# Three of the seven score tiles counted by signs on ScalarE in the search for the top-256 threshold

## The reference, cut to what matters

```python
score = jnp.where(admissible[None], score, NEG)
_, sel = lax.top_k(score, top_k)          # top_k = min(256, L // 4) = 256
k_sel, v_sel = _gather_rows(keys, sel), _gather_rows(vals, sel)
...
p = jax.nn.softmax(logits, axis=-1)
```

## Time and profile before

| what | value |
|---|---|
| median of three runs | 1867.98 us |
| the profiled execution's own time | 1866.54 us |
| its span, first to last instruction | 1864.7 us |
| busy: PE, DVE, ACT, POOL | 1761.9, 1216.4, 774.3, 372.8 us |
| mean granted TensorE clock | 0.984 |
| column tiles on TensorE | 164.9 to 469.5 us |
| the search | 165 to 346.6 us |
| q, k and v | 470 to 641 us |

### The profile page before, as it was taken

How to read it: one execution, slowest core, us unless ns; L and a number is a source line. 1 busy time by engine, 2 the same in 40 slices (tenths; PEclk the granted TensorE clock), 3 DMA queues, 4 the chain that set the end, 5 groups by cost and what they waited for, 6 DMA issues and landing times.

```text
span 1864.7 us, 30284 instructions
## 1 busy us (share of the span) xinstructions
PE 1761.9 (94%) x11736; PEld 1586.3 (85%) x11736; DVE 1216.4 (65%) x2156; ACT 774.3 (42%) x1664; POOL 372.8 (20%) x451
## 2 busy tenths in 40 slices
PE   6977999999999987998999999999999999999999
PEld 6935999999889854667988789999999999887877
DVE  4279898999999666765453577555565554444443
ACT  5377566412566267664122443322222222333332
POOL 2104322331784122330000001111111112000000
PEclk9999999999999998998999999999999999999999
DMA  6411112321212423784332213222222222657574
GB/s 199 72 54 35 46 40 82 108 94 62 81 52 69 148 63 132 256 282 189 134 119 79 79 52 93 73 72 72 71 77 72 77 72 94 214 173 237 174 239 154
DMA packets 92881, 209.23 MB, mean 112 GB/s; under 512 B 13333, under 2 KB 32693, under 8 KB 92483
## 3 DMA queue, kind: packets, MB, share of 16 engines
q1 hardware_dynamic: 86555, 193.26, 32.4%
q10 hardware_dynamic: 6192, 14.16, 1.9%
HBM read 167.77 MB, written 39.58 MB: 111 GB/s over the span
## 4 chain that ended last, share of the span: by engine, by line
PE 40%; issue 14%; DVE 3%; ACT 2%; DMA 1%; POOL 1%; SPq 1%; POOLq 0%; DVEq 0%; ACTq 0%
PE ps L823 12%; PE ps L825 12%; PE ps L824 12%; DVE buf L1678 1%; DMA buf<-f_scr 1%; PE ps L1071 1%; PE ps L1048 1%; ACT buf L1484 1%; DVE buf L2243 1%; DVE buf L1877 0%; PE ps L1061 0%; PE ps L1105 0%; PE ps L1090 0%; SPq L791 0%; ACT buf L1474 0%
## 5 line engine op out<-in xcount | busy, mean ns | idle before, releaser
L825 PE MATMUL ps<-buf,buf 128*128 128x288 f32 (+3 forms) x2660 | 877.1, 330 | 0.0
L824 PE MATMUL ps<-buf,buf 128*128 128x288 f32 (+3 forms) x2660 | 877.1, 330 | 0.0
L823 PE MATMUL ps<-buf,buf 128*128 128x288 f32 (+3 forms) x2484 | 828.5, 334 | 24.9 <-DVE buf L1678 17.5
L825 PEld LDWEIGHTS ps<-buf,buf 128*128 128x128 f32 (+1 forms) x2660 | 500.9, 188 | 24.5
L824 PEld LDWEIGHTS ps<-buf,buf 128*128 128x128 f32 (+1 forms) x2660 | 501.5, 189 | 23.6
L823 PEld LDWEIGHTS ps<-buf,buf 128*128 128x128 f32 (+1 forms) x2484 | 467.9, 188 | 53.1 <-DVE buf L1678 15.3
L1678 DVE TENSOR_TENSOR buf<-buf,buf 128x512 fp32r<-128x512 f32 (+5 forms) x363 | 322.4, 913 | 196.8 <-ACT buf L1669 123.9
L1825 DVE SCALAR_TENSOR_TENSOR buf<-buf,buf,buf 128x1024 f32<-128x1024 f32 x240 | 197.9, 866 | 4.0
L2390 POOL TENSOR_TENSOR buf<-buf,buf 128x288 f32<-128x288 f32 x88 | 78.9, 900 | 416.8 <-DVE buf L2113 375.2
L1764 DVE TENSOR_SCALAR_CACHE_REDUCE buf<-buf,buf 128x384 uint8<-128x384 f32 (+6 forms) x169 | 139.8, 888 | 1.2
L1005 PE MATMUL ps<-buf,buf 128*128 128x256 f32 x432 | 124.5, 288 | 0.6 <-ACT buf L1366 0.6
(11 more groups left out here) (202 smaller groups left out, 1949.4 us busy)
## 6 DMA issues: line engine op xcount, KB each, us to landing
buf<-in_w_ffn SPq DMA_DIRECT2D x66, 512.0 KB, 3.6
buf<-in_w_ffn SPq DMA_DIRECT2D x88, 256.0 KB, 2.7
buf<-in_cache_k SPq DMA_DIRECT2D x16, 1024.0 KB, 7.4
buf<-in_cache_v SPq DMA_DIRECT2D x16, 1024.0 KB, 10.5
f_scr<-buf SPq DMA_DIRECT2D x22, 576.0 KB, 4.2
buf<-f_scr SPq DMA_DIRECT2D x66, 192.0 KB, 3.9
buf<-in_w_cols SPq DMA_DIRECT2D x24, 512.0 KB, 3.9
buf<-in_x SPq DMA_DIRECT2D x18, 512.0 KB, 4.3
```

The source lines that it names most:

```text
L823: mm(dst, whi, xhi, start=start, stop=False)
L824: mm(dst, whi, xlo, start=False, stop=False)
L825: return mm(dst, wlo, xhi, start=False, stop=stop)
```

## The change

`NSIGN` becomes 3 and is defined earlier; three small vectors get three columns in place of two. So the tile of 896 keys (block 6) goes from VectorE's list to ScalarE's. ScalarE sums signs over 896, 1024 and 1152 keys in each of the 32 steps, VectorE counts over 384, 512, 640 and 768. After the last bit VectorE handles three tiles in lines 1791 to 1800, not two.

```diff
+        NSIGN = 3
...
-        kvec = take(2, o + 32)
-        diff = take(2, o + 40)
-        least = take(2, o + 48)
-        assert NSEL <= 8 and o + 50 <= o_gmix + D
+        kvec = take(NSIGN, o + 32)
+        diff = take(NSIGN, o + 40)
+        least = take(NSIGN, o + 48)
+        assert NSEL <= 8 and o + 48 + NSIGN <= o_gmix + D
...
-        NSIGN = 2
         signed = list(enumerate(select))[NSEL - NSIGN:]
```

## The result

The changed kernel takes 1870.04 us against 1867.51 (medians of 20 runs each): ratio 1.0014, 95% interval 1.0008 to 1.002, so 1.5 to 3.7 us slower. Forecast were 1871.1 us and a loss of 3.1. The profiled execution took 1870.4 us with a span of 1868.6, against 1866.54 and 1864.7.

What follows compares the result with a forecast made beforehand. TensorE was taken to bound the column stage, with ScalarE's lag using up the PSUM banks. Its 3.1 us loss, everything else costed at nothing, added to the 1867.98 median gives 1871.1 us; own range 1869.5 to 1873, wider range 1865.5 to 1877.

Steps and rivals of the forecast that it cites:

- What bounds the stage: Column stage: TensorE sets it, 25.2 us a GLU pair; ScalarE's lag just uses up six PSUM banks near 335 us.
- The cost of a sum: ScalarE, each search step: third sum over 896 keys adds 1.04 us plus a 0.12 gap, 1.16 us.
- Steps a, b, d and e: GLU pair's steps: a 3.26 to 4.42, b 4.80 to 4.42, d 4.74 to 4.42, e 10.06 to 11.22 us.
- the collision of c: GLU pair's third step: threshold update no longer falls beside GpSimd's low part, so 6.26 becomes 5.11 us.
- The loss of 3.1 us: Column tiles: TensorE loses 3.1 us once, in two or three small waits for ScalarE's late evacuations; bounds 0 and +8.
- step a of tile 8, at 281.84, stays where it is: Tile 8's first step: starts unmoved after four GLU pairs and takes 5.2 us beside GpSimd's product, as before.
- the first pair: First pair of GLU tiles: changes by -0.5 us, an estimate with bounds -1 and +1.2.
- rival 2: GLU pairs: update still meets GpSimd, c costs 7.4 us, a pair 2.8 more; 1876 to 1878 us, chance 0.2.
- The tail: VectorE after the last bit: some 2.9 us more work, masks and taps about 5.8 us later, covered, costing nothing.
- Rival 1: Column tiles: the lag is absorbed, evacuation at 335.18 late by less than 1; 1868.0 to 1868.9 us, chance 0.15.
- rivals 3 and 4: 3: later VectorE meets GpSimd less, 1864 to 1868, chance 0.1; 4: by occupancy, search 12 us shorter, 1867.5, chance 0.08.
- The signs: Expected: c at 5.1, VectorE waiting every step, copies ending about 307.6; wrong if a later stage changes over 1 us.

Runs made afterwards that it cites:

- kernels 3 and 8: Against the kernel before: 3, two tiles by signs in the search, three after the last bit, 1866.22 us; 8, that with its final count done twice, 1867.36 us.

## Why the prediction was right, step by step

- **What bounds the stage.** That TensorE sets it, with a reserve of six banks that is used up near 335 us, held: every kernel that eased ScalarE went to 304.4 to 305.4 us and has no wait for an evacuation left, and the one that burdened it further grew by 33.
- **The cost of a sum**, 1.04 us plus 0.12, held (1039 ns; sums start 1.17 apart). Steps a, b, d and e were right within 0.02 us, c within 0.09; the collision of c is gone, as worked out from the order.
- **The loss of 3.1 us** stands against 4.17 in the profiled stage, of which 0.8 is TensorE's clock at the start, so some 3.4 for the change (an estimate, by the first evacuations), and against 1.5 to 3.7 for the whole. The term that was wrong is "step a of tile 8, at 281.84, stays where it is", with its a step "5.2, as before". Tile 8 began 0.46 late: the first pair gained nothing (34.46 us from the first sum, against 34.16), where I had put -0.5. The missing 0.8 is the clock: the evacuation of 193.22 shown above waited 0.96 us for TensorE, and all that followed in the pair came after it. With the clock of the kernel before the pair would have gained some 0.5, as forecast (an estimate). What the forecast had wrong is the first step of tile 8, which took 6.05 us. With three sums the update came at 286.83, in the middle of GpSimd's product (285.98 for 2.40), and the first of its three instructions took 1.56 us:

```profile
286.83 1.56 DVE L1780 TENSOR_TENSOR buf<-buf,buf 128x3 f32<-128x3 f32 x1 [1.48 <-ACT buf L1350]
288.43 0.39 DVE L1781 TENSOR_SCALAR buf<-buf 128x3 int32<-128x3 f32 x1
288.85 0.17 DVE L1783 SCALAR_TENSOR_TENSOR buf<-buf,buf 128x7 int32<-128x7 int32 x1
```

  So rival 2 was right in kind at one place of one tile: 0.8 us. With the 0.5 by which tile 8 began late it makes the 1.3 us that the copies after tile 9 were later than forecast (2.44, not 1.16), and weight tile 12 took 0.2 longer to come; the gate steps gave 0.3 back. That the sum came so near is in part luck: the 0.8 of this meeting was not foreseen, and small gains in the second to fourth pair and in the gate steps (some 0.7 together) make up for most of it.
- **The tail** was sized at 2.9 us and took 5.3 more (19.89 us from the last update to the masks, against 14.62): four tiny operations stood beside GpSimd for 0.58 to 0.67 each, the first raise took 1.12. VectorE's first weight piece was 9.7 us late and not 5.8. It cost nothing, for the cover was large: the second piece started at 495.83, and by the last copy of the convolution (636.69 against 631.26) VectorE was 5.43 us late, as late as TensorE at its next stage (647.71 against 642.29). That kernels 3 and 8 lose nothing shows it.
- **Rival 1** fell with the stage, rivals 3 and 4 too: TensorE's waits for GpSimd in q, k and v went from 7.1 to 6.9 us, and the search ends at 350.67, 4.1 later, where the rule of occupancy gave 12 earlier. (In the earlier trace rows TensorE has the highest occupancy of all, 29.12 of 29.12 us, and it did bound the stage; the rule misled only in the choice between the two engines that hand the steps to each other.) The busy times of the pair, in the columns of the earlier trace rows, look like balance, with VectorE at 18.94 us and ScalarE at 22.68; but by the timeline ScalarE hardly waits for the update, and VectorE waits in every step.

```profile
200.35:229.85 29.50, 29.50 (x171) 29.50 (x171) 18.94 (x60) 22.68 (x39) 8.44 (x10) 1.00 0.13 36
```

- **The signs.** Most came: c took 5.02 us, VectorE waited in all 32 steps, and the copies after tile 9 ended at 309.53 (forecast 307.6, with 0.71 of it from the later start). One sign of being wrong came as well, a later stage that gives more than 1 us. After a pause of 2.08 us at the end of the product with the output weights, TensorE's clock falls in some executions and not in others. The stretch in the kernel before, in the changed one, and in the changed one again:

```profile
1065.40:1070.40 5.00, 4.96 (x19) 4.27 (x20) 5.00 (x5) 3.14 (x6) 0.00 (x0) 0.66 0.38 105
1072.10:1077.10 5.00, 4.95 (x26) 4.20 (x27) 5.00 (x5) 3.16 (x6) 0.00 (x0) 1.00 0.38 105
1072.40:1077.40 5.00, 4.92 (x19) 4.21 (x20) 5.00 (x6) 3.15 (x6) 0.00 (x0) 0.66 0.35 105
```

  From this pause to TensorE's next one (line 1161) it takes 26.2 us with the lower clock and 24.6 without, in variants of both kinds: 26.2 in the kernel before, the changed one again and with the second count, for example, 24.6 in the changed one and with the longer tail alone. So the 1.6 us between the two main profiles are chance and not the change.
- **What stays open.** The stage lost 4.2 us in both profiles, the whole program 2.5 (1.5 to 3.7) and 3.3 (0.7 to 4.1). Both profiles of the changed kernel had the late clock at the start, and that of the kernel before the early one. With 3.4 us for the change the two agree, but how often the clock is late in either kernel isn't known, for only profiled executions show it. The scatter of the stages behind is as large as the change: the clock explains the 1.6 us above, the rest isn't traced.

## What to carry to other kernels

Before work is moved from a busy engine to an idler one, write out one period of both engines' chains with their handshakes: the idler engine here had 40% idle time and yet the longest chain in two of five steps. New work is free as long as it fills that engine's own waits in such a step, and dear from then on (4.2 us for the first tile, 28.7 for the second). What a lag costs is decided by the reserve (here six PSUM banks), and reserve can be had back from any wait in the same engine's queue, such as a transfer queued behind an unrelated one. And before a difference of a microsecond between two profiles is put down to a change, compare the granted clock of TensorE behind each of its pauses: here it made 0.8 us at one place and 1.6 at another.

## What the runs showed of the hardware that was not expected

Tiny VectorE operations beside GpSimd's work cost far more than themselves: 0.58 to 0.67 us beside GpSimd's pieces of 0.7 us, and 1.56 us beside its product of 2.40 us, against 0.16 or 0.17 alone. They end about when GpSimd's current instruction ends: that of 286.83 at 288.39, GpSimd's product at 288.38. Counts kept their duration: over 896 keys one took 1.14 us at 175.83, beside GpSimd's first run, and 1.14 us at 344.71, where GpSimd stood still. The rows of the tiny operations agree with the rule of the Trainium skill, "GPSIMD Engine Reference", section "Key points", that the two engines contend for shared SBUF interfaces where VectorE's instruction runs in a 2-port mode or has two SBUF inputs. That of 1.56 us has two inputs; in which mode the others ran the rows don't say. It matters less how much GpSimd does than whether a chain of small handshakes falls into it.

TensorE's granted clock after a pause differs between executions of the same program: over the same 2.5 us of the column stage it was 0.75 and 1.00 in two kernels that don't differ up to there, and after a pause of 2.08 us it was 0.66 over 5 us in one profile of the changed kernel and 1.00 in the other.
